# Five norms of a decoder step: roots and reciprocals on a quarter of the tokens per 32 lanes, spread by products; and products of constants ahead of projections

## The chip, the cores and the metric

The kernel runs on one core of one Trainium2 chip. The metric is the device time of one launch in microseconds (us). The engines are called TensorE (PE in the profile, PEld for its weight loads), VectorE (DVE), ScalarE (ACT), GpSimd (POOL) and SyncE (SP, which issues most DMAs here). SBUF has 128 partitions, called lanes below; PSUM has 8 banks of 512 float32 per lane.

## What is computed

A two-layer decoder step on 576 tokens: 512 of one prompt and 64 samples (8 sequences of 8 tokens), with 1024 features, all in float32. Layer 1 is a gated linear recurrence, layer 2 is sliding-window attention with sinks, and each ends in a retrieval mixer over 16384 experts. What matters here is the norm, which stands five times on the path from input to output:

```python
def rmsnorm(x, g):
    xf = x.astype(jnp.float32)
    y = xf * lax.rsqrt(jnp.mean(xf * xf, axis=-1, keepdims=True) + EPS)
    return (y * g.astype(jnp.float32)).astype(x.dtype)

# trunk, in order of the norms (numbered 0 to 4 in the kernel):
# 0: recurrent_block(rmsnorm(x, rg_norm))         x = x + y
# 1: peer(rmsnorm(x, ffn_norm[0]))                x = x + ...
# 2: kv = rmsnorm(x, kv_norm) @ w_kv; q = rmsnorm(x, attn_norm) @ w_q   (one set of statistics)
# 3: peer(rmsnorm(x, ffn_norm[1]))
# 4: rmsnorm(x, final_norm)                        the output y
```

## The kernel before

**Layout.** The residual xT lies with features on the 128 lanes: 8 chunks (c = 0 to 7) of 128 features by 576 tokens. So a norm needs, for each token, a sum over lanes and chunks, and then the same factor for that token on every lane.

**A norm (number s).** ScalarE squares a chunk into xn (lines 642, 632). TensorE multiplies it by `ones`, a 128x128 matrix of 1/1024 (lines 1547, 1696, 1715), adding up the chunks in PSUM; the result is the mean of the squares, the same on all 128 lanes. ScalarE takes the root of all 576 tokens on all lanes into rinv (line 650, or 634 and 635), VectorE the reciprocal in place (line 935), and then VectorE makes each chunk's xn = xT * gain * rinv (line 948, `norm_apply`). ScalarE rounds xn to xh (line 662), VectorE makes the rest xl (line 941), two chunks behind its own xn, and TensorE begins the next projection with the chunk whose xl is there (`project_tile`, line 1563: products of high and low parts in two halves of 288 tokens). In norms 1 and 3 VectorE adds six of the chunks of squares beforehand (line 931), so that three chunks are left to TensorE: the sum of the six, chunk 6 and chunk 7.

**Norms 2 and 4** come at the end of an expert mixer, in `residual` (lines 1698 to 1720). TensorE folds the samples' part (line 1702), turns each chunk k of the output (four transposes, line 1710), VectorE adds it to xT (line 1361), ScalarE squares it (line 632), and TensorE sums it (line 1696, `prompt_sum`). The transposes of chunk k wait until VectorE has added chunk k - 3. The 64 samples' sums of all 8 chunks (line 1715) come after the transposes of chunk 4; after those of chunks 5, 6 and 7 one prompt sum each, and then the other five.

**Order and sharing.** Every engine works through its own list in program order; semaphores order them against each other. PSUM banks 0 to 3 hold the projections, banks 4 and 5 the sums of norms 0, 1 and 3, bank 4 and bank 7 those of norms 2 and 4. The expert mixer of each layer is two loops of 128 steps (`up`, line 1637, and `down`, line 1689), with gathered rows on VectorE beside them. The recurrence (about 86 to 185 us of the span) runs on VectorE and ScalarE, with the gate projections beside it; the attention (about 1657 to 1801 us) is a chain of small products, transposes, maxima, exponentials and copies over 16 units.

**What is column-tiled already.** Attention's sample scores (lines 1778 and 1779) multiply weights of 64 rows by 32 columns, and write to lanes 0, 32, 64 and 96 in turn; the mixer's sample scores (line 1626) have weights of 128 rows by 64 columns, writing twice to lane 0 and then twice to lane 64. Beside these, line 1616 does the same product with 128 columns of weights.

Of the kernel before, what the change touches and what calls it, by code (L numbers as in the profile page):

```python
# [236 lines left out]
def decoder(nc, xin, consts, params, wts, wv, stconv, kcT, kc, vc, uT, u, v,  # L237
            yT, convP, hOut, kNew, vNewP, vNewS, kKeep, vKeep, convS, gate_dram, s_dram):
    with ExitStack() as ctx:
# [13 lines left out]
        rinv = base.take("rinv", [P, T])  # L253
# [64 lines left out]
        prT = st.take("prT", [P, 2, 2 * GRP, P])  # L318
        pr = st.take("pr", [P, PRS, GRP, 2 * WIN])
        sm = st.take("sm", [P, PRS, 6, NB])  # L320
# [81 lines left out]
        SUM, SUMS = 4, 7  # L402
# [3 lines left out]
        sbP = ps[:, IOTA, KEYS + 2 * PH * TOPK:]  # L406

# [114 lines left out]
        def _(pool):  # L522
            pool.memset(eps[:, 0:1], EPS)
            pool.memset(ones[:, :], 1.0 / D).then_inc(sem("ones_ready"), 1)
            pool.memset(xpre[:, :, 0:CW - 1], 0.0).then_inc(sem("pad_ready"), 1)
# [94 lines left out]
        def _(act):  # L620
            def square(s):
# [3 lines left out]
                if s in (2, 4):  # L625
# [8 lines left out]
                    act.activation(rinv[:, TP:T], ps[:, SUMS, 0:SMP], ACT.Sqrt, bias=eps[:, 0:1])  # L634
                    act.activation(rinv[:, 0:TP], ps[:, SUM, :], ACT.Sqrt, bias=eps[:, 0:1]).then_inc(sem("rms_ready"), 1)
# [14 lines left out]
                act.activation(two(rinv[:, :]), halves(4), ACT.Sqrt, bias=eps[:, 0:1]).then_inc(sem("rms_ready"), 1)  # L650
# [214 lines left out]
            def attention():  # L865
                split_x(X_KV)
                rope_shift(D_K, 2)
# [55 lines left out]
        def _(dve):  # L923
# [20 lines left out]
            def norm_apply(off, k, lag=2):  # L944

                for c in range(NC + lag):
                    if c < NC:
                        dve.scalar_tensor_tensor(xn[:, c], xT[:, c], prm[:, off + c:off + c + 1],  # L948
                                                 rinv[:, :], ALU.mult, ALU.mult
                                                 ).then_inc(sem("x_whole" if k is not None else "y_ready"), 1)  # L950
                    if k is not None and c >= lag:
                        low_half(k, c - lag)
# [427 lines left out]
            def attention():  # L1380
# [8 lines left out]
                norm_apply(N_AT, X_AT)  # L1389
# [144 lines left out]
        def _(pe):  # L1534
            def sum_squares(s):
# [46 lines left out]
            def inputs():  # L1582

                project(W_IN, D_IN, NC, X_IN)
                for f in range(NC):
                    project_tile(W_GATE[f], D_GATE[f])
                    if f < 2:
                        rg_gates((W_A, W_X)[f], (D_A, D_X)[f])

            def outputs():  # L1590

                pe.wait_ge(sem("d_free"), D_OUT)
                pe.wait_ge(sem("out_split"), OUTS)
# [13 lines left out]
            def experts(l):  # L1607
# [86 lines left out]
                def prompt_sum(c):  # L1694
                    pe.wait_ge(sem("sq_ready"), SQ[2 * l + 2] + c + 2)
                    return pe.matmul(ps[:, SUM, :], ones[:, :], xn[:, c, 0:TP], start=(c == 0), stop=(c == NC - 1))

                def residual():
# [6 lines left out]
                    for k in range(NC):  # L1705
# [6 lines left out]
                        if k == 4:  # L1712
                            pe.wait_ge(sem("sq_ready"), SQ[2 * l + 2] + 1)
                            for c in range(NC):
                                pe.matmul(ps[:, SUMS, 0:SMP], ones[:, :], xn[:, c, TP:T],
                                          start=(c == 0), stop=(c == NC - 1))
# [4 lines left out]
                    ins.then_inc(sem("sum_done"), 1)  # L1721

# [24 lines left out]
            def attention():  # L1747
                project(W_K, D_K, 2, X_KV)
                pe.wait_ge(sem("wv_loaded"), 16)
                for t in range(TT):  # L1750
# [4 lines left out]
                ins.then_inc(sem("v_done"), 1)  # L1755
                project(W_Q, D_Q, NC, X_AT)
# [202 lines left out]
```

## Time and profile before

| | |
|---|---|
| median of 3 runs | 3200.64 us (3191.85 to 3200.99) |
| the profiled execution, its own time | 3202.49 us |
| its span, first to last instruction | 3200.7 us |
| TensorE busy | 3069.8 us (96%) |
| VectorE busy | 2551.4 us (80%) |
| GpSimd busy | 1746.1 us (55%) |
| ScalarE busy | 1382.4 us (43%) |
| mean granted TensorE clock | 0.972 of full |

Times in the profile are of one execution; about 1.8 us lie outside its span. A line L935 is line 935 of the kernel before. In the chain of waits the work that ended last is followed back from the last instruction, and each piece has its start, its length and what ran; in the timeline the instructions of one engine are merged by line. A float32 product shows as two records of TensorE, one of the fp32r products of the projections as one. The granted clock is 1.00 (2.4 GHz) or 0.50 (1.2 GHz) of full.

### The profile page before, as it was taken

To read this page: it belongs to the slowest core of one execution; us is meant where nothing else is said; L and a number is where in the kernel's file an instruction comes from. 1 tells how busy PE (TensorE), PEld (TensorE's weight loads), DVE (VectorE), ACT (ScalarE), POOL (GpSimd) and SP (SyncE) were. 2 spreads that over 40 slices of the span, in tenths; PEclk is the share of its full clock that TensorE was granted. 3 is DMA by queue.
4 is the path that set the end of the run, shared out by engine and by line. 5 is a ranking of instruction groups with operands and counts; after the bars stand their busy time and mean duration, and the time that the engine had idled before them with its cause. 6 is when DMAs were issued, how large, how long until landed. Compare 5 with 4: busy or idle time off the path is not lost.

```text
span 3200.7 us, 46734 instructions
## 1 busy us (share of the span) xinstructions
PE 3069.8 (96%) x17222; PEld 2780.8 (87%) x17222; DVE 2551.4 (80%) x4953; ACT 1382.4 (43%) x2559; POOL 1746.1 (55%) x1160
## 2 busy tenths in 40 slices
PE   7879999999999999999888889999999999999997
PEld 7879999999998888888685789999999988888886
DVE  7755999977775999999567358989877759999987
ACT  2522343477764333333344223343777653333332
POOL 4543488887775444443130223788877755544442
PEclk9989999999999999999887899999999999999998
DMA  3212499999999999999130022799999999999993
GB/s 106 77 53 91 128 340 337 339 397 393 393 392 373 401 400 399 401 397 351 53 95 1 27 67 80 274 348 342 371 400 387 395 370 394 399 401 400 398 400 138
DMA packets 286579, 920.92 MB, mean 288 GB/s; under 512 B 27344, under 2 KB 77392, under 8 KB 282688
## 3 DMA queue, kind: packets, MB, share of 16 engines
q1 hardware_dynamic: 154336, 415.63, 35.9%
q0 software_dynamic: 111280, 404.77, 33.4%
q10 hardware_dynamic: 20736, 97.53, 7.4%
q8 instruction: 138, 2.26, 0.3%
q14 instruction: 89, 0.73, 0.1%
HBM read 817.34 MB, written 102.38 MB: 287 GB/s over the span
## 4 chain that ended last, share of the span: by engine, by line
PE 77%; DVE 16%; DMA 3%; POOL 2%; issue 1%; ACT 1%; DVEq 0%; ACTq 0%; SPq 0%
PE ps L1689 34%; PE ps L1637 22%; PE ps L1563 11%; PE ps L1669 5%; POOL low L604 2%; DMA raw<-uT 1%; PE ps L1811 1%; DVE xn L948 1%; DVE xl L941 1%; DVE cand L1218 1%; DVE cand L1225 1%; DVE slot L1231 1%; PE ps L1765 1%; PE ps L1800 1%; DVE rowsB L1129 1%
## 5 line engine op out<-in xcount | busy, mean ns | idle before, releaser
L762 ACT ACTIVATE high<-raw 128x1024 fp32r<-128x1024 f32 x512 | 542.7, 1060 | 992.2 <-PE ps L1689 665.9
L1637 PE MATMUL ps<-xh,high 128*128 128x384 f32 x2048 | 699.1, 341 | 14.8 <-POOL low L604 14.6
L604 POOL TENSOR_TENSOR low<-raw,high 128x1024 fp32r<-128x1024 f32 x256 | 614.2, 2399 | 167.2 <-ACT high L762 160.5
L1637 PE MATMUL ps<-xh,low 128*128 128x384 f32 x2048 | 687.4, 336 | 0.0
L1637 PE MATMUL ps<-xl,high 128*128 128x384 f32 x2048 | 686.2, 335 | 0.0
L1689 PE MATMUL ps<-high,hh 128*128 128x512 f32 x1536 | 483.5, 395 | 7.9 <-DVE low L1301 7.9
L1689 PE MATMUL ps<-low,hh 128*128 128x512 f32 x1536 | 481.1, 394 | 0.0
L1689 PE MATMUL ps<-high,hl 128*128 128x512 f32 x1536 | 480.3, 393 | 0.0
L595 POOL DMA_INDIRECT rowsA<-v,pick x192 | 271.3, 1413 | 296.9 <-DVE ps L1136 288.8
L1637 PEld LDWEIGHTS ps<-xh,high 128*128 128x128 f32 x2048 | 386.1, 189 | 20.8 <-POOL low L604 19.8
L595 POOL DMA_INDIRECT rowsB<-v,pick x192 | 240.2, 1251 | 271.0 <-DVE ps L1136 255.6
L1637 PEld LDWEIGHTS ps<-xl,high 128*128 128x128 f32 x2048 | 386.0, 188 | 0.0
L1637 PEld LDWEIGHTS ps<-xh,low 128*128 128x128 f32 x2048 | 385.4, 188 | 0.0
L1689 PEld LDWEIGHTS ps<-high,hh 128*128 128x128 f32 x1536 | 288.5, 188 | 76.3 <-DVE low L1301 8.5
L1689 PEld LDWEIGHTS ps<-low,hh 128*128 128x128 f32 x1536 | 287.9, 187 | 70.9
L1689 PEld LDWEIGHTS ps<-high,hl 128*128 128x128 f32 x1536 | 288.5, 188 | 69.1
L1301 DVE TENSOR_TENSOR low<-raw,high 128x1024 fp32r<-128x1024 f32 x256 | 312.3, 1220 | 0.0
L1563 PE MATMUL ps<-xh,high 128*128 128x288 f32 x1152 | 257.5, 306 | 50.4 <-DVE xl L941 41.7
L1129 DVE SCALAR_TENSOR_TENSOR rowsB<-rowsB,ps 128x1024 f32<-128x1024 f32 x192 | 231.0, 1214 | 45.6 <-DMA rowsB<-u,pick 44.5
L1563 PE MATMUL ps<-xl,high 128*128 128x288 f32 x1152 | 252.5, 302 | 0.0
L1563 PE MATMUL ps<-xh,low 128*128 128x288 f32 x1152 | 252.4, 301 | 0.0
L1129 DVE SCALAR_TENSOR_TENSOR rowsA<-rowsA,ps 128x1024 f32<-128x1024 f32 x192 | 230.8, 1213 | 21.6 <-DMA rowsA<-u,pick 14.1
(279 smaller groups left out, 5043.5 us busy)
## 6 DMA issues: line engine op xcount, KB each, us to landing
raw<-uT SPq DMA_DIRECT2D x256, 512.0 KB
raw<-v SPq DMA_DIRECT2D x256, 512.0 KB
gate_dram<-gblk ACTq DMA_DIRECT2D x24, 2048.0 KB
gt<-gate_dram SPq DMA_DIRECT2D x32, 1536.0 KB
s_dram<-sring ACTq DMA_DIRECT2D x120, 384.0 KB
sring<-s_dram SPq DMA_DIRECT2D x120, 384.0 KB
raw<-wts SPq DMA_DIRECT2D x74, 512.0 KB, 3.6
rowsB<-u,pick POOLq DMA_INDIRECT x192
```

The costliest lines, as they stand in the source:

```text
L595: pool.indirect_dma_start(out=row_slot(k), out_offset=None, in_=u if k < S0 + S1 else v, in_offset=bass.IndirectOffsetOnAxis(ap=pick[:, c: ...
L604: pool.tensor_tensor(low[:, m % 4], raw[:, m % 4], high[:, (m + 2) % 3].bitcast(F32), ALU.subtract).then_inc(sem("lo_ready"), 1)
L762: act.activation(high[:, (m + 2) % 3], tile_raw(m), ACT.Copy).then_inc(sem("hi_ready"), 1)
L941: dve.tensor_tensor(xl[:, c], xn[:, c], xh[:, c].bitcast(F32), ALU.subtract).then_inc(sem("xl_ready"), 1)
L948: dve.scalar_tensor_tensor(xn[:, c], xT[:, c], prm[:, off + c:off + c + 1], rinv[:, :], ALU.mult, ALU.mult).then_inc(sem("x_whole" if k is ...
L1129: dve.scalar_tensor_tensor(row, row, 1.0, wide(XS0 if k < S0 else XS1), ALU.mult, ALU.mult, accum_out=phid[:, c:c + 1]).then_inc(sem("row_ ...
L1218: chain.did(dve.tensor_tensor(eq[a], cabf[:, a, 0:nh].unsqueeze(3).broadcast_to([P, nh, TOPK, TOPK]), iotaP[:, 0:TOPK].unsqueeze(1).unsque ...
L1301: dve.tensor_tensor(tile_low(m), tile_raw(m), high[:, (m + 2) % 3].bitcast(F32), ALU.subtract).then_inc(sem("vlo_ready"), 1)
L1563: ins = pe.matmul(ps[:, dbank(d) + h, 0:H2], m[:, c], x[:, c, h * H2:(h + 1) * H2], start=(c == 0 and j == 0), stop=(c == NC - 1 and j == 2))
L1637: ins = pe.matmul(ps[:, m % 2, 0:DN], w[:, c], x[:, c, 0:DN], start=(c == 0 and k == 0), stop=(c == NC - 1 and k == 2))
L1669: ins = pe.matmul(ps[:, 2 + g % 2, i * P:(i + 1) * P], hotB[:, k], hotA[:, k], start=True, stop=True)
L1689: ins = pe.matmul(ps[:, YC[c] + d, :], h[:, n % 3, c * P:(c + 1) * P], w[:, d * 512:(d + 1) * 512], start=(n == 0 and i == 0), stop=(n == ...
```

## The change

- The sums are multiplied by `ones[:, 0:32]` and written by quarters: the tokens 0 to 143 (of 576) to lanes 0 to 31 of bank 6, tokens 144 to 287 to lanes 32 to 63, and so on. A chunk now has four products of 144 tokens instead of two of 288. In norms 2 and 4 a prompt chunk has four products of 128 tokens instead of one of 512, and a sample chunk four of 16 instead of one of 64 (32 products instead of 8).
- ScalarE takes the root of 144 columns into rq in one instruction (before: 576, in norms 2 and 4 as 64 and 512), and VectorE the reciprocal of 144.
- TensorE spreads rq to all lanes (`spread`): with pickq, four 128x128 matrices of zeros with a row of ones at lane 32q, four products of 144 columns into banks 4 and 5 (norms 0, 1, 3), or nine, of 128, 32, 96 and 16 columns (norms 2 and 4). GpSimd makes pickq at the start (one memset of 128x512 and four of 128 columns on one lane, each waiting for the one before).
- `norm_apply` reads the factor from PSUM. For the second use of norm 2's statistics ScalarE copies it to rinv, now in space of the attention (576 columns, after `split_x(X_KV)`); the products for V wait for that copy, since they write to banks 4 to 6.
- `keep_warm(n, bank)`: n float32 products of 512 columns of constants, whose result nobody reads. One after the sums and two after the spread in norms 0 to 3, two before the seventh gate projection, two before the recurrent block's output projection (after a wait for a PSUM bank, ahead of the wait for its weights), and two between V and the queries.

```diff
-                act.activation(two(rinv[:, :]), halves(4), ACT.Sqrt, bias=eps[:, 0:1]).then_inc(sem("rms_ready"), 1)
+                act.activation(rq[:, :], ps[:, SUM, 0:T // 4], ACT.Sqrt, bias=eps[:, 0:1]).then_inc(sem("rms_ready"), 1)
...
             def norm_stats(s):
                 dve.wait_ge(sem("rms_ready"), s + 1)
-                chain.did(dve.reciprocal(rinv[:, :], rinv[:, :]))
-                chain.settle()
+                dve.reciprocal(rq[:, :], rq[:, :]).then_inc(sem("rq_ready"), 1)
+                dve.wait_ge(sem("rinv_ready"), s + 1)
...
+            def keep_warm(n, bank):
+
+                for _ in range(n):
+                    pe.matmul(ps[:, bank, :], ones[:, :], prm[:, P_SK:P_SK + 4 * KEYS], start=True, stop=True)
+
+            def spread(s):
+
+                if s == 0:
+                    pe.wait_ge(sem("pick_ready"), 4)
+                    pe.wait_ge(sem("params_loaded"), 16)
+                if s < 4:
+                    keep_warm(1, WARM)
+                pe.wait_ge(sem("rq_ready"), s + 1)
+                if s in (2, 4):
+                    n = TP // 4
+                    parts = [(q, 0, n, q * n) for q in range(4)] + [
+                        (q, n, n + SMP // 4, TP + q * SMP // 4) for q in range(4)]
+                else:
+                    parts = [(q, 0, T // 4, q * T // 4) for q in range(4)]
+                for q, lo, hi, t in parts:
+                    cut = min(max(H2 - t, 0), hi - lo)
+                    for a, b in ((lo, lo + cut), (lo + cut, hi)):
+                        if a < b:
+                            at = t + a - lo
+                            o = at % H2
+                            ins = pe.matmul(ps[:, RINV + at // H2, o:o + b - a], pickq[:, q], rq[:, a:b],
+                                            start=True, stop=True)
+                ins.then_inc(sem("rinv_ready"), 1)
+                if s < 4:
+                    keep_warm(2, WARM)
...
-                    for h in range(2):
-                        ins = pe.matmul(ps[:, 4 + h, 0:H2], ones[:, :], xn[:, c, h * H2:(h + 1) * H2],
-                                        start=(c == 0), stop=(c == NC - 1))
+                    for q in range(4):
+                        ins = pe.matmul(quarter(SUM, q, 0, T // 4), ones[:, 0:32],
+                                        xn[:, c, q * T // 4:(q + 1) * T // 4], start=(c == 0), stop=(c == NC - 1))
                 ins.then_inc(sem("sum_done"), 1)
+                spread(s)
```

## Rows read from the trace of the kernel before

**Rows 1.** The page's part 4, the chain that ended last, by engine:

```profile
PE 77%; DVE 16%; DMA 3%; POOL 2%; issue 1%; ACT 1%; DVEq 0%; ACTq 0%; SPq 0%
```

**Rows 2.** Chain of waits, norm 0: start us, us, what:

```profile
7.05 10.40 PE ps L1547 x32
...
18.39 3.77 DVE rinv L935
22.18 2.95 DVE xn L948 x3
```

**Rows 3.** Timeline of SP and POOL, norm 0: start us, us, engine, line, what:

```profile
1.64 0.43 SPq L415 DMA_DIRECT2D prm<-params  x1
...
17.30 2.34 POOL L582 TENSOR_TENSOR low<-raw,high 128x1024 fp32r<-128x1024 f32 x1
```

**Rows 4.** DMA issues, 0 to 60 us: KB each, median us from issue to landing:

```profile
prm<-params SPq DMA_DIRECT2D x1, 352.5 KB, 13.4
```

**Rows 5.** Chain of waits, norm 1:

```profile
226.55 1.28 ACT L650
...
232.40 2.28 DVE xn L948 x3
```

**Rows 6.** Chain of waits, norm 2, end of the residual and the roots:

```profile
1545.15 1.73 PE ps L1715 x16
...
1549.48 0.44 PE ps L1710 x4
1549.92 5.17 PE ps L1696 x12
...
1555.42 0.59 ACT rinv L635
```

**Rows 7.** Chain of waits, norm 3:

```profile
1855.33 2.92 PE ps L1547 x12
```

**Rows 8.** Timeline of ACT, norm 3:

```profile
1856.75 1.04 ACT L656 ACTIVATE high<-raw 128x1024 fp32r<-128x1024 f32 x1
```

**Rows 9.** Groups by line and form: xcount | busy us, mean ns | idle before:

```profile
L935 DVE RECIPROCAL rinv<-rinv 128x576 f32<-128x576 f32 x5 | 18.8, 3753 | 35.4 <-ACT rinv L650 24.8 <-ACT rinv L635 10.6
L1428 DVE RECIPROCAL sm<-sm 128x4 f32<-128x4 f32 x16 | 2.9, 178 | 0.5
L650 ACT ACTIVATE rinv<-ps,eps 128x576 f32<-128x576 f32 x3 | 2.2, 741 | 3.4 <-PE ps L1547 3.4
L634 ACT ACTIVATE rinv<-ps,eps 128x64 f32<-128x64 f32 x2 | 0.6, 315 | 7.6 <-PE ps L1696 7.6
L1361 DVE TENSOR_TENSOR xT<-xT,ps 128x512 f32<-128x512 f32 x16 | 10.8, 687 | 6.1 <-PE ps L1710 6.1
L632 ACT ACTIVATE xn<-xT 128x512 f32<-128x512 f32 x16 | 10.0, 630 | 6.8 <-DVE xT L1361 6.6
L1129 DVE SCALAR_TENSOR_TENSOR rowsB<-rowsB,ps 128x1024 f32<-128x1024 f32 x192 | 231.0, 1214 | 45.6 <-DMA rowsB<-u,pick 44.5 <-issue 0.8
L1301 DVE TENSOR_TENSOR low<-raw,high 128x1024 fp32r<-128x1024 f32 x256 | 312.3, 1220 | 0.0
```

**Rows 10.** Groups by line and form, attention's sample scores (64 rows, 32 columns):

```profile
L1778 PE MATMUL ps<-kc_sb,qS 64*32 64x128 f32 x64 | 4.4, 410 | 0.0
```

**Rows 11.** Stretch of those scores, PE: us, busy (records), PEclk, DMA, GB/s:

```profile
1678.85:1683.34 4.49, 4.49 (x130) 0.50 0.00 0
```

**Rows 12.** Chain of waits, layer 1's mixer, scores with 128 and 64 columns:

```profile
266.90 6.39 PE ps L1563 x48
273.29 0.89 PE ps L1616 x8
274.18 0.60 PE ps L1626 x8
274.77 6.57 PE ps L1563 x48
```

**Rows 13.** Attention: PE, PEld, DVE, ACT, POOL busy, then PEclk, DMA, GB/s:

```profile
1691.20:1801.00 109.80, 93.60 (x388) 56.48 (x387) 73.25 (x143) 42.70 (x125) 0.00 (x0) 0.80 0.00 1
```

More of the change, by code:

```diff
@@ L252, in decoder @@
         prm = base.take("prm", [P, P_N])
-        rinv = base.take("rinv", [P, T])
+        rq = base.take("rq", [P, T // 4])
+        pickq = base.take("pickq", [P, 4, P])
         ones = base.take("ones", [P, P])
@@ L318, in decoder @@
         prT = st.take("prT", [P, 2, 2 * GRP, P])
+        pr_at = st.at
         pr = st.take("pr", [P, PRS, GRP, 2 * WIN])
+        rinv = Span(nc, pr_at, SB_HI).take("rinv", [P, T])
         sm = st.take("sm", [P, PRS, 6, NB])
@@ L401, in decoder @@
         OUT, OUTS_B = 6, 7
-        SUM, SUMS = 4, 7
+        SUM, RINV, WARM = 6, 4, 7
         iotaP = ps[:, IOTA, 0:KEYS]
@@ L406, in decoder, with quarter @@
         sbP = ps[:, IOTA, KEYS + 2 * PH * TOPK:]
+        def quarter(bank, q, lo, hi):
+            return ps[32 * q:32 * q + 32, bank, lo:hi]
         block = ctx.enter_context(nc.Block())
@@ L866, in attention @@
                 split_x(X_KV)
+                act.activation(two(rinv[:, :]), halves(RINV), ACT.Copy).then_inc(sem("rinv_kept"), 1)
                 rope_shift(D_K, 2)
@@ L942, in low_half, with norm_apply @@
                                   ).then_inc(sem("xl_ready"), 1)
-            def norm_apply(off, k, lag=2):
+            def norm_apply(off, k, lag=2, inv=None):
+                inv = halves(RINV) if inv is None else two(inv)
                 for c in range(NC + lag):
                     if c < NC:
-                        dve.scalar_tensor_tensor(xn[:, c], xT[:, c], prm[:, off + c:off + c + 1],
-                                                 rinv[:, :], ALU.mult, ALU.mult
+                        dve.scalar_tensor_tensor(two(xn[:, c]), two(xT[:, c]), prm[:, off + c:off + c + 1],
+                                                 inv, ALU.mult, ALU.mult
                                                  ).then_inc(sem("x_whole" if k is not None else "y_ready"), 1)
@@ L1388, in attention @@
                 dve.memset(mark[:, :], 0.0).then_inc(sem("k_ready"), 2)
-                norm_apply(N_AT, X_AT)
+                dve.wait_ge(sem("rinv_kept"), 1)
+                norm_apply(N_AT, X_AT, inv=rinv[:, :])
                 rope(D_Q, NC, qR)
@@ L1585, in inputs @@
                 for f in range(NC):
+                    if f == 6:
+                        keep_warm(2, 6)
                     project_tile(W_GATE[f], D_GATE[f])
@@ L1695, in prompt_sum @@
                     pe.wait_ge(sem("sq_ready"), SQ[2 * l + 2] + c + 2)
-                    return pe.matmul(ps[:, SUM, :], ones[:, :], xn[:, c, 0:TP], start=(c == 0), stop=(c == NC - 1))
+                    for q in range(4):
+                        ins = pe.matmul(quarter(SUM, q, 0, TP // 4), ones[:, 0:32],
+                                        xn[:, c, q * TP // 4:(q + 1) * TP // 4], start=(c == 0), stop=(c == NC - 1))
+                    return ins
                 def residual():
@@ L1714, in residual @@
                             for c in range(NC):
-                                pe.matmul(ps[:, SUMS, 0:SMP], ones[:, :], xn[:, c, TP:T],
-                                          start=(c == 0), stop=(c == NC - 1))
+                                for q in range(4):
+                                    pe.matmul(quarter(SUM, q, TP // 4, T // 4), ones[:, 0:32],
+                                              xn[:, c, TP + q * SMP // 4:TP + (q + 1) * SMP // 4],
+                                              start=(c == 0), stop=(c == NC - 1))
                         if k >= 5:
@@ L1721, in residual @@
                     ins.then_inc(sem("sum_done"), 1)
+                    spread(2 * l + 2)
                 if l == 0:
```

11 lines of the change are left out of this document (9 added, 2 removed).

## The prediction

> **What bounds the kernel now.** I read the page's chain of waits first, then the same chain in order of time around each of the five norms, then the timelines of the engines there, then the groups by form for prices. The chain is TensorE's for 77% [rows 1], so nearly everything downstream of a norm starts when TensorE may, and time taken out of a norm should pass on whole. At the norms the chain leaves TensorE: the reader is to see a reciprocal of 3.77 us on VectorE, alone, with TensorE waiting [rows 2]; there are five, each 3753 ns [rows 9]. Ahead of it stand the root on ScalarE (741 ns in norms 0, 1 and 3 [rows 9]) and, in norms 0, 2, 3 and 4, TensorE's sums; norm 2's last six prompt sums alone take 5.17 us [rows 6]. Norm 4's chain has the same pieces as norm 2's.
>
> **Root and reciprocal.** VectorE's reciprocal goes with columns, not lanes: 178 ns for 4, 3753 for 576 [rows 9], so 6.25 ns a column, and 144 columns take 178 + 140 x 6.25 = 1.05 us. Saved per norm: 2.70 us. The root takes 315 ns for 64 columns and 741 for 576 [rows 9], 0.83 ns a column, so 0.38 for 144: saved 0.36 in norms 0, 1 and 3. In norms 2 and 4 two roots stand one behind the other, 0.32 [rows 9] and 0.59 [rows 6]: saved 0.53.
>
> **The spread, new on the path.** A float32 record of 512 columns takes 5.17/12 = 0.43 us at full clock [rows 6], so 144 columns 0.12, a product of two records 0.24, four 0.97. With 0.3 for the two hand-overs and the last product's way through the array (an estimate: steps between engines in the chains are up to 0.14 us) this is 1.27 us in norms 0, 1 and 3. Norms 2 and 4 have nine products, short ones; sixteen records of 64 columns (line 1715) took 1.73 us [rows 6], 0.108 each, however short, so 18 take 1.95, 2.25 with the 0.3. At half clock the products double: 2.25 and 4.2 us. I take full clock for norms 1 to 4, since TensorE has worked until about 2 us before, and half for norm 0.
>
> **The sums: tiles of 32 columns side by side.** One answer would be that nothing is gained: the same columns pass, in four products for two. The trace says otherwise. Attention's sample scores write to four groups of 32 lanes in turn: 64 records of 128 columns [rows 10], and as many of 8, took 4.49 us at a clock of 0.50 [rows 11]. A record of 128 columns takes 0.89/8 = 0.11 us at full clock [rows 12] and twice that at half, so the 64 alone would need 14 in a row. Done in a third of that, the four groups ran side by side. With 128 rows of weights it holds too: eight records of line 1626, 64 columns wide, took 0.60 us, those of line 1616, 128 wide, 0.89 [rows 12]. So I price a chunk's four quarters as one: 0.24 us for 144 columns (before 0.97), 0.22 for 128 (before 0.86).
>
> For the 32 sample products (64 records of 16 columns) the bounds are 64/4 x 0.027 = 0.43 us (time by columns only, a quarter of a 64-column record) and 4.49/128 x 64 = 2.2 us (the spacing of records in rows 11). I take 1.7, toward the row that has narrow records in it; that is what the eight of 64 columns take now [rows 6]. The Trainium skill, "TensorEngine Tiling (Array Packing)", Instruction Overhead, gives each matmul some 60 cycles however few its columns, which by itself would put 64 records at 1.6 us. The same page's Key Properties say that changing the tiling mode drains TensorE. Behind the tiled scores the next 48 records take 6.57 us instead of 6.39 [rows 12], 0.18 for the way back; I take 0.2 for each change.
>
> What that gives by norm:
> - Norm 0. Now the reciprocal ends and xn starts at 22.18 [rows 2]. The sums (10.40 us from 7.05 [rows 2]) need a quarter of that and end with the last squares; later than these is ScalarE's wait for the parameters: issued at 1.64 [rows 3], landed 13.4 later [rows 4], 15.04. Then root 0.38, reciprocal 1.05, hand-overs 0.1, spread 2.25: xn at 18.85. Saved 3.3 (4.3 at full clock). The first weights are split at 17.30 + 2.34 = 19.64 [rows 3], before the first xl at about 22, so they stay hidden.
> - Norm 1. ScalarE loads the root's table until 227.83 [rows 5], after the sums are done; only what follows is shorter: 0.36 + 2.70 - 1.27 = 1.8.
> - Norm 2. After the sample sums (1.7 for 1.73) come three rounds of transposes (0.44 each [rows 6]), two of them followed by a sum (0.22) and its change of mode (0.2): 1545.15 + 1.7 + 1.3 + 0.85 = 1549.0. Then VectorE adds chunk 7 (0.69), ScalarE squares it (0.63) [rows 9] and one sum is left (0.3): 1550.65 instead of 1555.09. Saved 4.4 (5.6 with the cheap sample sums, 3.9 with the dear). With root and reciprocal: 4.4 + 0.53 + 2.70 - 2.25 = 5.4.
> - Norm 3. The sums end at 1858.25 [rows 7]; with tiles they would end about 0.25 after the last square, which is over before ScalarE begins a split of weights at 1856.75 [rows 8]; the end of that split, 1857.79, is the next bound. Saved 0.45 + 1.8 = 2.25.
> - Norm 4 as norm 2: 5.4.
>
> Sum: 3.3 + 1.8 + 5.4 + 2.25 + 5.4 = 18.2 us.
>
> **Edits that I cost at nothing.** VectorE reads the factor from PSUM: a scalar_tensor_tensor of 1024 with a PSUM operand takes 1214 ns, one without, 1220 [rows 9]; 0. The constant product before the spread (0.86 at full clock) ends before rq, 1.5 us after the sums; the two behind (1.7 us, 3.4 at half) lie under VectorE's three xn (2.28 us [rows 5]) and a first xl of some 0.7, 3 us; at half clock 0.4 would show once. The projection's head is paced by VectorE (an xn of 0.76 us [rows 5] and an xl of about as much for each chunk, some 1.4, against 6 x 6.39/48 = 0.8 for TensorE at full clock [rows 12] and 1.6 at half), so a warm TensorE gains at most 0.3 there. The pairs before the gates and the output projection lie where VectorE's recurrence is the chain. ScalarE's copy of rinv (0.74, as the root of 576 [rows 9]) lies under the two projections for K (2 x 6.39 [rows 12]); V's products, which wait for it, and all that is queued behind them on TensorE come after those. GpSimd's memsets come before its first split of weights, which waits for a load until about 16 us [rows 3]. If a cover is gone, each edit costs what is named with it, under 1 us.
>
> **Total.** 3202.49 - 18.2 = 3184.3 for the profiled execution; it lies 1.85 us over the median of the runs shown, so 3182.4.
>
> **Rivals.**
> 1. *The quarters run one after the other* (weights of 128 rows unlike those of 64). Then norms 0, 1 and 3 give 1.8 each, and norms 2 and 4 0.53 + 2.70 - 2.25 = 1.0 less up to 64 x 0.108 - 1.73 = 5.2 for the sample sums. Together from 7.4 saved to 3 lost: 3193 to 3204. I take narrow records at half of 0.108, 1.7 lost in each of the two: 3197. The 0.60 us for half-wide products speak against it [rows 12].
> 2. *Half clock at the ends.* The residual has less work on TensorE, its clock falls, and the spreads of norms 1 to 4 cost 0.97, 1.95, 0.97 and 1.95 more, and two of the three rounds of transposes in norms 2 and 4 0.44 more each: 7.6 us in all, so 3190. For it: three quarters of the sums' work is gone, so TensorE pauses between chunks where it didn't. Against: norms 1 and 3 follow on unbroken projections.
> 3. *The gain is not passed on*: a transfer that keeps its time holds a later stage up. 3200. Against it: loads are issued when TensorE or GpSimd frees a buffer, so they move along.
> 4. *Slower: attention's clock.* Its products run at 0.80 of full on the mean with 93.6 of 109.8 us busy [rows 13], so 40% of that stretch is at half clock, and which part depends on how the pauses fall. The change shifts all of it by some 10 us. Each us that goes from full to half costs up to 0.85 us; 22 us more of it, of the 66 at full, would eat the 18 us, and beyond that it is slower: 3205 at 28 us. Equally it may fall the other way.
>
> **Chances.** Forecast 0.66, rival 2 0.13, rival 1 0.10, rival 3 0.05, rival 4 0.06 (0.05 of it past its 22 us). The range: downward the forecast with the cheap sample sums twice (2.4), norm 0 at full clock (1.0) and attention's clock in its favour (the three runs before spread over 9 us): 3169. Upward rival 2 and the better end of rival 1: 3194. That leaves out most of rivals 1, 3 and 4 and a little below, 0.18. Faster by over 0.3% (below 3191; a measurement of this kernel can't tell less from no change) holds for the forecast and nearly all of rival 2, 0.78; within 0.3% rivals 1 and 3 and some of rival 4, 0.17; slower 0.05.
>
> **What would show it.** In the profile after: a reciprocal of 144 columns at 1.05 us (if it were 3.75, time would go with lanes); the four quarters' records of a chunk starting within 0.1 us of each other; norm 2's root 4 us behind its sample sums, where it now begins 8 behind; spreads of 1 and 2 us at a granted clock of 1.00; xn at 0.73 us a chunk as before. If the sums' records follow one another, rival 1; if the granted clock is 0.50 at the spreads, rival 2; if all that holds and the time doesn't, the attention's granted clock is where to look.

## The result, and the profile after

The changed kernel takes 3178.03 us (median of 6 runs, 3172.37 to 3187.83); the kernel before, on the same chip, 3202.58 (6 runs, 3191.85 to 3216.10). The ratio is 0.993, with a 95% interval of 0.9912 to 0.9948: about 22 us, 0.7%, faster. A second measurement of the same kernel gave 0.9944 (0.9925 to 0.9963). The forecast was 3182.4. The profiled execution took 3180.52 us, with a span of 3178.7, 22.0 shorter than before.

Line numbers have moved: the root is now L662 (L647 in norms 2 and 4), the reciprocal L948, the spread L1574, xn L961, xl L954; the sums are L1592 (norms 0, 1, 3), L1746 (prompt) and L1768 (samples), the constants L1552, the transposes of the residual L1762, its fold L1754.

The page's part 4 of the kernel after, the answer to [rows 1]:

```profile
PE 72%; DVE 19%; DMA 4%; POOL 2%; issue 1%; ACT 1%; SPq 0%; DVEq 0%; ACTq 0%; POOLq 0%
```

TensorE's share went from 77% to 72, and 5% of the span is 160 us, far more than the norms. It is the mixers: between 350 and 1000 us the scores' line had 63.1% of the chain before and has 47.3% now; VectorE, GpSimd and transfers have the rest. The length of that stretch is read below.

Groups by line and form of the kernel after, the answer to [rows 9]: xcount | busy us, mean ns | idle before:

```profile
L948 DVE RECIPROCAL rq<-rq 128x144 f32<-128x144 f32 x5 | 5.3, 1053 | 21.6 <-ACT rq L662 18.5 <-ACT rq L647 3.1
L961 DVE SCALAR_TENSOR_TENSOR xn<-xT,prm,ps 128x576 f32<-128x576 f32 x40 | 31.0, 807 | 8.6 <-PE ps L1574 8.6
L961 DVE SCALAR_TENSOR_TENSOR xn<-xT,prm,rinv 128x576 f32<-128x576 f32 x8 | 6.3, 812 | 0.0
```

The reciprocal is 1053 ns instead of 3753, as its columns say. An xn with the factor in PSUM (807 ns) costs what one with the factor in SBUF costs (812).

Chain of waits of the kernel after, norm 2, from the end of the mixer's output to the first xn; the answer to [rows 6]: start us, us, what:

```profile
1538.07 3.65 PE ps L1754 x16
1541.71 3.72 PE ps L1762 x20
1545.43 0.67 PE ps L1768 x52
1546.10 0.59 PE ps L1762 x4
1546.68 0.36 PE ps L1746 x8
...
1548.60 0.70 DVE xT L1374
...
1550.01 0.47 PE ps L1746 x8
...
1550.50 0.39 ACT rq L647
...
1550.98 1.06 DVE rq L948
...
1552.09 2.20 PE ps L1574 x18
...
1554.31 2.26 DVE xn L961 x3
```

A chunk's prompt sum is now 0.36 us with its change of mode where it was 0.86, and the root begins 5.1 us behind the start of the sample sums, where it was 10.0. The six prompt sums in a row of [rows 6] are gone from the chain: five of them now run while VectorE and ScalarE work on the last chunk. That the four quarters run side by side shows in their starts. Timeline of the kernel after, 1546.605 to 1546.640 us:

```profile
1546.61 0.32 PE L1746 MATMUL ps<-xn,ones 128*32 128x128 f32 x4
```

Four records of about 0.3 us each start within 0.02 us, and the next four 0.13 us later.

Stretches of TensorE: us, busy (records), PEclk, DMA, GB/s. First the kernel before, norm 2 and norm 4 (end of the mixer's loop to the first xn), attention, and the two mixers (first score to first output product):

```profile
1535.22:1559.89 24.67, 17.31 (x81) 0.83 0.26 86
3166.95:3191.47 24.52, 17.23 (x81) 0.82 0.00 1
1660.63:1801.18 140.55, 119.59 (x584) 0.73 0.08 23
356.26:998.37 642.11, 631.62 (x3916) 1.00 0.95 357
1986.71:2630.20 643.49, 631.30 (x3916) 1.00 0.95 356
```

The same five of the kernel after:

```profile
1535.53:1554.31 18.78, 15.42 (x197) 0.82 0.37 113
3154.01:3169.53 15.52, 11.14 (x195) 1.00 0.00 1
1654.99:1789.11 134.12, 111.42 (x584) 0.79 0.08 24
350.87:998.72 647.85, 634.16 (x3916) 0.99 0.95 353
1970.98:2616.86 645.88, 633.25 (x3916) 0.99 0.95 355
```

With norms 0, 1 and 3 this accounts for the span (us; positive is saved). Norm 0 is taken at the first gate product (86.53, now 82.86), norms 1 and 3 from the last product before to the first xn.

| | forecast | this execution |
|---|---|---|
| norm 0 | 3.3 | 3.7 |
| norm 1 (8.60 to 6.84) | 1.8 | 1.8 |
| norm 2 (24.67 to 18.78) | 5.4 | 5.9 |
| norm 3 (7.77 to 5.41) | 2.25 | 2.4 |
| norm 4 (24.52 to 15.52) | 5.4 | 9.0 |
| five norms | 18.2 | 22.7 |
| attention | 0 | 6.4 |
| output projection behind it (53.89 to 52.66) | 0 | 1.2 |
| layer 0's mixer | 0 | -5.7 |
| layer 1's mixer | 0 | -2.4 |

The sum is 22.2 for the 22.0 that the span became shorter. The experiments ask three things: what carries the gain in the norms, whether an earlier start passes on through the mixers, and which rows of this table repeat.

### The profile page after: what moved, and what is told of

The parts are those of the page before. It is cut to its first block, busy times and chain, and to the rows that moved or that the text cites. A ratio compares the mean times of both kernels' runs of the same rounds, so it can differ in the third digit from the quotient of the medians.

```text
span 3178.7 us, 47428 instructions
## 1 busy us (share of the span) xinstructions
PE 3063.7 (96%) x17566; PEld 2767.5 (87%) x17566; DVE 2544.9 (80%) x4953; ACT 1381.5 (43%) x2558; POOL 1743.8 (55%) x1165
## 4 chain that ended last, share of the span: by engine, by line
PE 72%; DVE 19%; DMA 4%; POOL 2%; issue 1%; ACT 1%; SPq 0%; DVEq 0%; ACTq 0%; POOLq 0%
PE ps L1738 33%; PE ps L1686 18%; PE ps L1609 11%; PE ps L1718 5%; POOL low L617 2%; DMA raw<-uT 1%; DVE rowsB L1142 1%; DVE cand L1231 1%; DVE cand L1238 1%; DVE xl L954 1%; DVE rowsA L1142 1%; DVE xn L961 1%; DVE slot L1244 1%; PE ps L1868 1%; DMA gate_dram<-gblk 1%
## 5 line engine op out<-in xcount | busy, mean ns | idle before, releaser
L608 POOL DMA_INDIRECT rowsA<-v,pick x192 | 259.5, 1352 | 305.0 <-DVE ps L1149 299.2
L608 POOL DMA_INDIRECT rowsB<-v,pick x192 | 247.4, 1288 | 271.3 <-DVE ps L1149 252.7
L1609 PE MATMUL ps<-xh,high 128*128 128x288 f32 x1152 | 254.7, 303 | 26.5 <-DVE xl L954 17.9
L816 ACT ACTIVATE sring<-ps 128x384 f32<-128x384 f32 x256 | 125.0, 488 | 299.4 <-PE ps L1686 298.7
```

The lines of the kernel that those rows point to most:

```text
L608: pool.indirect_dma_start(out=row_slot(k), out_offset=None, in_=u if k < S0 + S1 else v, in_offset=bass.IndirectOffsetOnAxis(ap=pick[:, c: ...
L816: act.activation(sring[:, p % 4, m % 2], ps[:, m % 2, 0:DN], ACT.Gelu).then_inc(sem("g_up"), 1)
L1609: ins = pe.matmul(ps[:, dbank(d) + h, 0:H2], m[:, c], x[:, c, h * H2:(h + 1) * H2], start=(c == 0 and j == 0), stop=(c == NC - 1 and j == 2))
```

## The experiments

All are edits of the changed kernel. Ratios are to the kernel before on the same chip, with their 95% intervals.

| kernel | median us (range, runs) | ratio |
|---|---|---|
| the changed kernel again | 3181.82 (3181.18 to 3189.93, 5) | 0.9944 (0.9925 to 0.9963) |
| no_constants | 3181.62 (3178.0 to 3186.98, 5) | 0.9940 (0.9917 to 0.9962) |
| sums_untiled | 3203.86 (3194.36 to 3214.29, 10) | 1.0016 (1.0001 to 1.0031) |
| norm1_late_5 | 3186.09 (3177.85 to 3193.26, 6) | 0.9946 (0.9931 to 0.9961) |
| norm1_late_16 | 3197.91 (3187.56 to 3210.72, 7) | 0.9984 (0.9964 to 1.0003) |
| second_split_late | 3180.80 (3170.14 to 3189.84, 5) | 0.9935 (0.9922 to 0.9948) |
| attention_constants | 3178.53 (3177.14 to 3180.17, 4) | 0.9920 (0.9905 to 0.9934) |
| quarters_grouped | 3182.99 (3176.85 to 3189.43, 5) | 0.9935 (0.9907 to 0.9963) |
| even_quarters | 3180.02 (3171.85 to 3184.24, 6) | 0.9916 (0.9891 to 0.9941) |
| even_and_warm | 3182.75 (3177.01 to 3185.0, 6) | 0.9928 (0.9904 to 0.9952) |

**The two kernels again.**

> The kernel before, unchanged, for a second profile. The five norms of the changed kernel's profile account for some 19 to 20 us of the 22 between the two spans; the rest is a sum of larger gains and losses elsewhere: layer 0's mixer lost 5.7 us, attention gained 6.5, layer 1's mixer lost 2.8. Theory A (these are how pauses and transfers fall in one execution): in this second profile of the same kernel the same stretches differ from the first by several us either way, while every norm keeps its length to 0.1 us (3.77 us for each reciprocal, 5.17 for norm 2's last sums). Theory B (they belong to the change): the stretches repeat to within 1 us. Time: 3200 +- 8.

> The changed kernel, unchanged, for a second profile. Theory A: norm 0 to 4 repeat (xn of norm 0 at 15.8 us of the span, the spreads 1.3 and 2.2 us), attention and the two mixers differ from the first profile of it by several us. Theory B: attention 6.5 us shorter than before and layer 0's mixer 5.7 longer, again. Time: 3178 +- 6.

> The kernel before once more, for a third profile. Attention (first scores to output projection) took 140.6 and 139.0 us in its two profiles, at a granted clock of 0.73 and 0.75, and 133.2 to 135.1 in seven of the eight of the other kernels (139.1 in one), at 0.77 to 0.83. Theory (chance: attention's clock depends on how its pauses fall in an execution): 134 or 139, either may come, and no part of the gain is to be put down to it. Rival (the change moves it for good): 139 to 141 again.

The first of these texts has 19 to 20 us for the five norms and 2.8 for layer 1's mixer; read from the same two profiles by the table above they are 22.7 and 2.4.

The kernel before against itself gave 1.0003 (0.9988 to 1.0019) and 0.9995 (0.9976 to 1.0014). The changed kernel's second profile is the more useful, since it shows which rows of the table above are the change's and which are one execution's. Its norm 4 and its attention, in the columns of the stretches above:

```profile
3157.25:3176.05 18.80, 14.42 (x194) 0.82 0.00 1
1652.68:1791.81 139.13, 117.65 (x585) 0.75 0.08 23
```

Norm 4 took 18.8 there, 5.7 less than before, at the granted clock that it also had before (0.82). In the first profile the clock was 1.00, which is the other 3.3 us: the fold and the transposes took 3.61 and 3.84 us here, and in the first profile, by its chain of waits:

```profile
3156.55 1.97 PE ps L1754 x16
3158.52 2.19 PE ps L1762 x20
```

Attention was as long as before (139.1). In the two further profiles of the kernel before it took 139.0 and 139.3; the third was what the rival of its expectation asked for, and what the theory allowed too. Norm 1 saved 0.7 instead of 1.8, since its spread ran at half clock. The mixers took 647.1 and 645.5.

**Tiling alone.** The sums go back to 128 columns of weights and two halves; root, reciprocal and spread stay on quarters (the roots pick each quarter from its own 32 lanes).

```diff
-                    for q in range(4):
-                        ins = pe.matmul(quarter(SUM, q, 0, T // 4), ones[:, 0:32],
-                                        xn[:, c, q * T // 4:(q + 1) * T // 4], start=(c == 0), stop=(c == NC - 1))
+                    for h in range(2):
+                        ins = pe.matmul(ps[:, SUM + h, 0:H2], ones[:, :], xn[:, c, h * H2:(h + 1) * H2],
+                                        start=(c == 0), stop=(c == NC - 1))
...
-                act.activation(rq[:, :], ps[:, SUM, 0:T // 4], ACT.Sqrt, bias=eps[:, 0:1]).then_inc(sem("rms_ready"), 1)
+                for q in range(4):
+                    o = q * T // 4
+                    ins = act.activation(rq[32 * q:32 * q + 32, :],
+                                         ps[32 * q:32 * q + 32, SUM + o // H2, o % H2:o % H2 + T // 4],
+                                         ACT.Sqrt, bias=eps[32 * q:32 * q + 32, 0:1])
+                ins.then_inc(sem("rms_ready"), 1)
```

> The changed kernel with the sums as before (weights of 128 columns, all tokens on all lanes, in banks 6 and 7) and the root taken from them in four instructions of 32 lanes each (eight in norms 2 and 4), so that root, reciprocal and spread stay on a quarter. My theory (a chunk's four quarters run side by side): the sums take back 4.4 us in norm 0, 0 in norm 1, 4.4 in norms 2 and 4, 0.45 in norm 3, and the added roots about 1.1 us in each of norms 0, 1, 3 and 2.2 in 2 and 4: 21 us more, 3199. Rival (quarters one after the other, so tiles save nothing): the added roots alone, 7.7 us, 3186.

It took 22.0 us more than the changed kernel beside it, and isn't faster than the kernel before. Chain of waits of sums_untiled, norm 2:

```profile
1546.00 1.73 PE ps L1775 x16
...
1550.77 5.17 PE ps L1756 x12
...
1555.96 0.36 ACT rq L649
```

The 5.17 of [rows 6] is back. Norm 2 took 27.2 us instead of 18.8. Of these 8.4 us the sums are 4.9 (the root 10.0 behind the sample sums' start instead of 5.1), the eight roots 1.7 (2.1 for 0.39), and the spread 1.7 (3.86 for 2.20), since it ran at a granted clock of 0.53; norm 4 took 27.1, with a spread of 3.88. So not all of the 22 is the sums', and some of it is a clock that the expectation hadn't counted. But rival 1, quarters one after the other, falls: its 3186 didn't come, and the starts above show them side by side. And a reciprocal of 1.05 us, by itself, gains nothing in this form: the spread and the four or eight roots eat it. The tiles save twice, in the sums and by letting one root do.

**Constants.**

```diff
-                for _ in range(n):
+                for _ in range(0):
```

> The changed kernel without the products of constants. My theory (they hide and buy next to nothing, since VectorE paces the head of each projection): 3178, within 3 us of the changed kernel; the spreads of norms 1 to 3 may come at half clock and cost 1 to 2 us each at worst. Rival (the surplus over the forecast is theirs: a warm TensorE through spread, projection head and what follows): 3184 to 3186, with the granted clock at 0.50 in the spreads of norms 0 to 3 (0.97 + 0.97 + 1.95 + 0.97 us) and in the first 3 to 7 us of the queries' projection (1.2 us).

3181.62 against 3181.82. The products of constants are worth nothing that can be measured. Whether they act on the clock differs by place. The spread of norm 1, chain of waits of no_constants:

```profile
224.50 2.30 PE ps L1574 x8
```

and of the kernel after:

```profile
225.81 1.26 PE ps L1574 x8
```

Norm 3's spread took 2.30 without them too, and 1.26 in all ten profiles with them. In norm 1 they are no guarantee: with one product ahead of it the spread took from 1.26 to 2.30 in eight profiles, 2.30 in the changed kernel's second. The price is 1 us where it falls.

**Is an earlier start passed on?** In the first profiles layer 0's output loop began at nearly the same time in both kernels (998.4, 1000.0 before; 998.7, 997.9 after), though its scores began 5.4 us earlier. That would make norms 0 and 1 worthless. So norm 1 is made late by 5 and by 16 us, with more constant products:

```diff
-                    keep_warm(1, WARM)
+                    keep_warm(10 if s == 1 else 1, WARM)
```

and with 23 in place of 10.

> The changed kernel with ten products of constants instead of one ahead of norm 1's spread, so that norm 1's factor and all behind it come about 5 us later, near where the kernel before has it. In the six profiles so far layer 0's down loop starts between 997.9 and 1000.0 us of the span, whether its up loop starts at 350.6 or at 356.3. Theory A (the mixer of layer 0 takes up what norms 0 and 1 give): the up loop starts 5 us later, the down loop still near 998.5, and the time is that of the changed kernel, 3181 +- 3. Theory B (the gains of norms 0 and 1 pass on, and the agreement was chance): down loop near 1003, 3186.

> As norm1_late_5 with 23 products, so that all behind norm 1 comes 16 us later than in the changed kernel, 11 us later than in the kernel before. Theory A with a fixed point that doesn't move with the up loop: down loop at 998.5 again, or as much later as its own minimum length (638 to 644 us seen) demands: 361.5 + 638 + 4 = 1010 at most 5 us less than a full shift. Theory B: stretch from up to down 644 to 648 us as in the changed kernel, down loop at 1014, 3197.

Chain of waits of norm1_late_16:

```profile
222.26 19.94 PE ps L1552 x46
...
243.22 2.26 DVE xn L961 x3
```

xn begins 16.2 us later than in the changed kernel. The time is 16.1 us above 3181.8, or 13 to 17 by the ratios. With 5 us (xn at 231.21, 4.2 later) it is 4.3 above, 1 to 5 by the ratios. In the profiles the output loop began at 995.9 (5 us) and 1012.2 (16 us). The first fits neither theory, being earlier than the 997.9 and 998.7 of the changed kernel; the second lies between the 1010 that a fixed point allowed and the 1014 of a full shift (the 361.5 in that expectation is wrong: the scores began at 367.0, and a shortest mixer of 638 with the 4 us would end at 1009). So one profile can't decide it, and the times do: most or all of the 16 us is passed on, and full absorption falls. Their intervals leave room for some us. The equal times were chance: the mixer's own length differs from execution to execution. For layer 0 it was 642.1, 643.8 and 643.2 in three profiles of the kernel before, 647.8 and 647.1 in two of the changed one, and 640.1 to 649.3 in nine variants of it. For layer 1: 643.5, 642.4, 642.3; 645.9, 645.5; 639.9 to 649.3. No variant touches the mixer. It has gathered rows on its chain; in layer 0 of the kernel after one piece of the chain is a wait of 9.7 us for them (at 573.7).

**Norm 0.** Its xn started 6.3 us earlier than before (15.84 for 22.18), but the gates only 3.7. The chain of waits of the kernel after shows where:

```profile
13.03 0.31 ACT rq L662
...
15.84 2.26 DVE xn L961 x3
18.10 2.30 DVE xl L954
20.41 0.72 DVE xn L961
21.13 0.79 DVE xl L954
21.92 0.72 DVE xn L961
22.64 2.13 DVE xl L954
```

Two xl take over 2 us instead of 0.67. Timeline of GpSimd in the same stretch: start us, us, engine, line, what:

```profile
17.44 2.35 POOL L595 TENSOR_TENSOR low<-raw,high 128x1024 fp32r<-128x1024 f32 x1
19.73 1.57 POOL L593 CAST high<-raw 128x1024 fp32r<-128x1024 f32 x1
21.39 2.76 POOL L595 TENSOR_TENSOR low<-raw,high 128x1024 fp32r<-128x1024 f32 x1
```

GpSimd's instructions end at 19.79, 21.30 and 24.15, and the xl that stand beside them end at 20.40, 21.92 and 24.77: each about 0.6 us later, the length of one xl. They don't share; the xl does nothing until GpSimd's instruction is over. In the timelines of the changed kernel and its variants 29 xl of norm 0 took over 0.8 us, from 0.81 to 2.92, and all of them end 0.61 or 0.62 us behind an instruction of GpSimd. To see whether that is the cause, GpSimd's second split waits until five xl are done:

```diff
+                    if w == 1:
+                        pool.wait_ge(sem("xl_ready"), 5)
```

> The changed kernel with GpSimd's split of the second weight tile waiting for the fifth xl of norm 0. In the changed kernel's profile three xl of norm 0 take 2.39, 0.86 and 2.20 us where others take 0.75, while GpSimd splits weights; xn, which reads PSUM, stays at 0.80. My theory (VectorE and GpSimd hold each other up on SBUF, and that eats 2.5 of the 6 us that norm 0 gives): the later xl take 0.75 us, the first tile's end comes 1 to 2 us sooner; in the time at most 2 us less, if layer 0's mixer passes it on. Rival (the slow xl wait for ScalarE's xh, not for GpSimd): the same 2.2 us without GpSimd beside it, and the first tile ends where it did or later.

Timeline of second_split_late, VectorE and then GpSimd:

```profile
18.52 1.59 DVE L956 TENSOR_TENSOR xl<-xn,xh 128x576 fp32r<-128x576 f32 x1
20.04 0.80 DVE L963 SCALAR_TENSOR_TENSOR xn<-xT,prm,ps 128x576 f32<-128x576 f32 x1
20.77 0.74 DVE L956 TENSOR_TENSOR xl<-xn,xh 128x576 fp32r<-128x576 f32 x1
...
26.34 4.59 DVE L956 TENSOR_TENSOR xl<-xn,xh 128x576 fp32r<-128x576 f32 x3
```

```profile
17.14 2.37 POOL L597 TENSOR_TENSOR low<-raw,high 128x1024 fp32r<-128x1024 f32 x1
...
26.89 2.76 POOL L597 TENSOR_TENSOR low<-raw,high 128x1024 fp32r<-128x1024 f32 x1
```

The first xl again ends 0.6 after GpSimd's instruction (20.11 after 19.51). While GpSimd stands still, the next four take 0.74 to 0.75; the last three meet the moved split and take 4.59 together, where they took 2.08. The xn beside them stays at 0.80: it reads two streams too, but one from PSUM. So the cause holds, but the sooner end of 1 to 2 us didn't come, since the cure only moves the cost: the gates began at 83.2, the time is the same. The Trainium skill ("SBUF — State Buffer", SBUF: two separate sides) states this as a rule: GpSimd and a VectorE instruction with two SBUF inputs contend for one shared pair of ports, and it is "an exclusive lock, not a bandwidth split". These traces agree, with up to 2.9 us in the timelines for 0.75 in an xl that came second; weighed against the change, which moved the xl onto GpSimd's splits, the rule would have given norm 0's loss.

In the changed kernel's second profile GpSimd started its splits 0.9 us earlier, only one xl was held for long (2.12), and the gates began at 81.80, 4.7 before the 86.50 of before_again.

And why was xn 6.3 earlier and not 3.3? The forecast made the root wait for the parameters until 15.04. In the three profiles of the kernel before they landed at 14.9 to 15.0, in all eleven profiles of the changed kernel and its variants at 9.9 to 12.9. What the change moved there is GpSimd's own transfer, which now stands behind the memsets for pickq. Timelines of GpSimd, before and after:

```profile
1.39 2.96 POOL L526 DMA_DIRECT2D xpreS<-stconv  x1 [0.36 <-issue]
```

```profile
2.58 2.96 POOL L539 DMA_DIRECT2D xpreS<-stconv  x1
```

So it was issued ahead of the parameters (1.64) before, and is issued behind them (1.65) now. The second half of the input landed earlier too, at 8.9 to 9.2 instead of 10.2 to 10.7. That the order of issue is the cause fits all fourteen profiles, but no run changes it alone. With tiled sums the root then began at 12.8 to 13.0 in all ten profiles, right behind ScalarE's squares and the 1.28 us of loading its table, even where the parameters had landed at 9.9. ScalarE is the bound there now.

**Attention.** Its clock was rival 4. One constant product of 256 columns ahead of each unit's turn:

```diff
-                    pe.wait_ge(sem("p_ready"), u + 1)
                     if u:
...
+                    pe.matmul(ps[:, 2, 0:256], ones[:, :], prm[:, P_SK:P_SK + 256], start=True, stop=True)
+                    pe.wait_ge(sem("p_ready"), u + 1)
```

> The changed kernel with one product of constants of 256 columns (0.43 us at full clock) ahead of each of the 16 turns of attention. In the six profiles attention's granted clock is 0.73 to 0.80 and the stretch from its first scores to the output projection 133 to 141 us, shorter where the clock is higher. Theory (its clock falls where TensorE pauses for VectorE, and that is what varies between executions): the clock rises to 0.9 or more and the stretch falls to 125 to 130: 3172. Rival (pauses aren't what sets it; the small products with 64 rows are): clock 0.75 to 0.80, and the stretch is longer by up to 16 x 0.43 = 7 us: 3188.

The stretch of attention in attention_constants:

```profile
1648.80:1783.92 135.12, 117.48 (x616) 0.83 0.08 24
```

The mean clock is 0.83, where the changed kernel's two profiles had 0.79 and 0.75, and the stretch, 135.1, lies between their 134.1 and 139.1. Perhaps the added products (16 x 0.43 = 6.9 us at most) filled what the clock gave; no run shows it. Neither theory comes out clean. Over all profiles attention took 139.0 to 140.6 in three of the kernel before, 134.1 and 139.1 in the changed one, and 133.2 to 137.2 in its variants, seven of the nine under 135.2. The means are 139.6 for the three and 135.1 for the eleven. That looks as if the change moved attention by some 4 us, but nothing was done that shows what does it; it stays open.

**Narrow products.** The forecast was dear for the 32 sample sums (1.7 us; measured 0.67). Is that the taking of turns between the four groups of 32 lanes? The same products, ordered by quarter:

```diff
-                            for c in range(NC):
-                                for q in range(4):
+                            for q in range(4):
+                                for c in range(NC):
```

> The changed kernel with the 32 sample products of norms 2 and 4 in another order: all eight chunks of a quarter one behind the other, then the next quarter, instead of the four quarters of a chunk in turn. Same products, same results. In the changed kernel's profile the 64 records take 0.67 us, 10 ns each, where I had forecast 1.7. Theory (it is the turn-taking between four groups of 32 lanes that makes narrow records cheap; one group alone takes 4 x 10 = 42 ns or more a record): 64 x 0.042 = 2.7 us or more, the roots of norms 2 and 4 each 2 us or more later, 3185. Rival (narrow weights make a record cheap by themselves, whatever the order): 0.7 us again, 3181.

Chain of waits, norm 2, of quarters_grouped:

```profile
1540.70 1.83 PE ps L1768 x64
```

That is 28.6 ns a record where in turn it is 10.5 (0.67 us; the trace holds all 64, though the chain counts 52). From start to start it is 27.2 ns on the mean against 8.8. Turns matter, less than the 42 ns expected, and 1.1 us in each of two norms doesn't show in the time.

Then the layout: with 144 tokens in each quarter in norms 2 and 4 too (the last has 80 of the prompt and the 64 samples), the sample sums are 8 products and the spread 4.

```diff
-                if s in (2, 4):
+                if False:
...
-                                for q in range(4):
-                                    pe.matmul(quarter(SUM, q, TP // 4, T // 4), ones[:, 0:32],
-                                              xn[:, c, TP + q * SMP // 4:TP + (q + 1) * SMP // 4],
-                                              start=(c == 0), stop=(c == NC - 1))
+                                pe.matmul(quarter(SUM, 3, TP - 3 * T // 4, T // 4), ones[:, 0:32],
+                                          xn[:, c, TP:T], start=(c == 0), stop=(c == NC - 1))
```

> The changed kernel with the same quarters in norms 2 and 4 as in the others (tokens 0 to 143 and so on): a prompt chunk has four products of 144, 144, 144 and 80 columns, a sample chunk one of 64, and the spread four products of 144 columns instead of nine. Theory: the spreads of norms 2 and 4 take 1.26 us instead of 2.20, the sample sums (16 records of 64 columns to one group of lanes) between 0.7 and 1.7 us instead of 0.67; together up to 0.9 us a norm: 3179 to 3181, not to be told from the changed kernel by time, but by the profile. Rival (the spread's records go by columns, so nine cost what four do): no difference in the spread.

> even_quarters with the product of constants ahead of norm 4's spread too. In the profiles of the changed kernel and its variants norm 4's reciprocal to xn takes 3.33 us where the clock is full (changed kernel, second_split_late) and 4.66 where it is half (no_constants, norm1_late_5). Theory: with 0.9 us less spread and full clock 2.4 us each time, the best version so far, 3178 to 3181. Rival: the clock at that point is set by the residual's pauses before it, and one product changes nothing.

Chain of waits, norm 2, of even_quarters:

```profile
1540.52 1.01 PE ps L1768 x16
...
1547.60 1.26 PE ps L1574 x8
```

The spread is 0.94 shorter, the sample sums 0.34 longer, so 0.6 us in each of two norms. Its ratio, 0.9916, is the lowest of all, but its interval overlaps those of the changed kernel, and so does that of even_and_warm, which adds the constant ahead of norm 4's spread. Norm 4's spread took 1.26 us in both, without the constant and with it, so it bought nothing in these profiles. Neither is shown to be better, and the 3178 to 3181 expected of the second was missed (3182.75).

## Why the prediction was right

**Root and reciprocal, spread and PSUM operand.** 0.39, 1.06, 1.26 and 2.20 us against 0.38, 1.05, 1.27 and 2.25 priced; xn unchanged. The prices held, within 0.05 us each, at full clock.

**The sums.** Pricing a chunk's quarters as one held: their records start within 0.02 us of each other, and without the tiles the whole gain is gone (sums_untiled). Inside it three sizes were off and cancel in part in norm 2. The sample sums were 0.67, not 1.7: I went toward the spacing of rows 11 (35 ns a record), which was taken at half clock with records of 128 columns in it, and the low bound, 0.43, was much nearer. The three transposes with their two sums took 2.5, not 2.15 (each change of mode about 0.15, and it lies on all three rounds). The last sum was 0.47, not 0.3. Sum: root 5.1 behind the sample sums' start, forecast 5.5. (With the cheap bound the saving would by the prediction's own terms have been 5.7, not 5.6.)

**Norm 0.** Forecast 3.3, kept 3.7, by luck: two errors partly cancel. xn was 6.3 earlier, since the root began at 12.96 and not 15.04, and since the spread ran at full clock, 1.26 for 2.25 (it did in seven of eleven profiles). The root's start isn't one execution's: the parameters and the input landed earlier in every profile with the change in it. I had costed GpSimd's memsets at nothing, and they come ahead of its transfer. Then VectorE's xl met GpSimd's splits: 2.39, 0.86 and 2.20 in the timeline for three times 0.75, 3.2 us, less the 0.7 that the xn no longer lose. I had written that these "stay hidden", looking only at when the weights are ready. The clue was in my own rows: three xn took 2.95 in norm 0 [rows 2] and 2.28 in norm 1 [rows 5]. The 0.67 more is the same contention, with the factor still in SBUF and GpSimd in its second split; in sums_untiled, where xn starts at the same time (22.29) beside the same split but reads the factor from PSUM, the three take 2.27. I didn't ask why the row differs from its twin.

**Norms 1 and 3** as forecast, to 0.1, when the spread has full clock.

**Norm 4.** Forecast 5.4, measured 9.0 and 5.7. The term that I left out is the clock of what lies ahead of the sums: fold and transposes ran at half clock before (3.65 and 3.66), and in one execution at full (1.97 and 2.19). In the five variants whose norm 4 is the same the stretch took 17.2 to 20.0, at mean clocks between 0.75 and 0.90. So 15.5 to 20.0 belongs to this stage; rival 2 named half clock at spread and transposes only, and no gain from the clock.

**Rival 2** came true in single places: norm 1's spread in one of two executions, norm 4's (3.53 in no_constants). One spread at half clock cost 1.0 us in norm 1 (priced 0.97), and in norms 2 and 4 1.3 to 1.7 (no_constants and sums_untiled; priced 1.95).

**Rival 3** is refuted in its full form: most or all of a late start is passed on. **Rival 4**, attention's clock, moved in the good direction if at all. The edits costed at nothing cost nothing that shows, and one of them, as norm 0 tells, seems to have gained some 2 us.

**What stays open.** In the two profiles of the changed kernel the norms gave 22.7 and 20.9 us (against the first profile of before 4.7, 0.7, 7.4, 2.4 and 5.7 for the second), and the two mixers were together 7.9 and 6.8 longer than the mean of three profiles before. A mixer's length varies by 9 us among kernels that don't touch it. Over the eleven profiles of the changed kernel and its variants the two together take 1288.7 on the mean, in the three before 1285.8, so whether the change lengthens them by some 3 us isn't settled, and neither is attention's part. The norms thus gave 4.5 and 2.7 us more than the 18.2 forecast, and that the time came so near (22 us by the first ratio, 17.9 by the second) is in part chance.

## What to carry to other kernels

A product with `ones` whose result is the same on all lanes does the same work four times over: with 32 columns of weights and four lane groups in turn, the sums cost about 0.4 of what they did here (0.36 us for 0.86, 0.67 for 1.73), and everything behind them (root, reciprocal) works on a quarter of the columns; the spread back costs four products. Without the tiled sums, and so with four or eight roots, it didn't pay here. When a stage starts earlier, look at what the other engines do in the stretch that it moves into, and ask of every row that is longer than its twin elsewhere why it is.

## What the runs showed of the hardware

- 64 records of 16 columns, in turn over four groups of 32 columns of the array, took 0.67 us at full clock, 10.5 ns a record, and 8.8 ns from one start to the next on the mean. In groups of 16 to the same lanes they took 1.83 us, 28.6 ns a record, and 27.2 from start to start. The Trainium skill ("TensorE: Matmul & The Clock Gate", Wait — 56ns, not 53.3ns?) says that start-to-start never drops below about 25 ns. The trace agrees, on the mean, for records to one group and differs for groups in turn.
- A VectorE TENSOR_TENSOR of two SBUF operands (0.67 us in the chain) that came upon a running TENSOR_TENSOR or cast of GpSimd ended 0.61 or 0.62 us after it in all 29 cases of norm 0 in ten profiles, however long that was: up to 2.9 us. GpSimd's own took 2.76 instead of 2.35 there, and its cast 1.57 instead of 1.03. The VectorE instruction with one operand in PSUM wasn't slowed.
- The granted clock after the same work isn't the same from one execution to the next: norm 1's spread, 2.22 us after TensorE's last product, took 1.26 us in one profile of the changed kernel and 2.30 in the other.
